# A hybrid decoder step: the chunk preparation reordered, and the sample's attention in f32r high and low parts

## The reference

```python
h = rmsnorm(x, norm_g); proj = h @ w_in            # (tokens, 1024) @ (1024, 4104)
qkv = silu(conv4(proj_a)); o_a = gated_delta_rule(q, k, v, g, beta, s0)   # 4 heads of 128, chunked
# sample's window attention, 8 heads of 64: per query t, the keys at distances 0, d, 2d, ...
parts = [dilated_branch_sample(qb, k_ext, v_ext, w // d, d) for w, d in ((128, 1), (512, 4), (2048, 16))]
o_b = merge_dilations(parts) * silu(z_b)
y = rmsnorm(x + concat(o_a, o_b) @ w_out, final_norm_g)
```

## Time and profile before

| what | value |
|---|---|
| the profiled execution's own time | 2152.05 us |
| its span, first to last instruction | 2149.3 us |
| mean granted PE clock | 0.916 |
| PE busy | 1883.7 us, 88% |
| DVE, ACT, POOL busy | 756.7, 596.1, 319.4 us |
| DMA moved | 310.31 MB, mean 144 GB/s |

### The profile page before, as it was taken

How to read it: one execution, slowest core, us unless ns; L and a number is a source line. 1 busy time by engine, 2 the same in 40 slices (tenths; PEclk the granted TensorE clock), 3 DMA queues, 4 the chain that set the end, 5 groups by cost and what they waited for, 6 DMA issues and landing times. The chain is left out here.

```text
span 2149.3 us, 29657 instructions
## 1 busy us (share of the span) xinstructions
PE 1883.7 (88%) x9726; PEld 1471.0 (68%) x9726; DVE 756.7 (35%) x1780; ACT 596.1 (28%) x1246; POOL 319.4 (15%) x351
## 2 busy tenths in 40 slices
PE   5799999999999999854659998998899559899997
PEld 4588888888888888623457887787788436555653
DVE  5541134113411431124465344444442422222331
ACT  5421132113211321111014534453445212211221
POOL 0000000000000000014313124312432331211110
PEclk9899999999999999976859888988899559999999
DMA  6234423354553234459855987797756475546560
GB/s 167 53 69 93 101 66 68 104 88 60 79 103 81 63 74 113 77 74 232 235 142 178 288 244 231 237 290 235 241 176 215 141 190 152 156 138 167 139 190 25
DMA packets 263857, 310.31 MB, mean 144 GB/s; under 512 B 69596, under 2 KB 216540, under 8 KB 254252
## 3 DMA queue, kind: packets, MB, share of 16 engines
q1 hardware_dynamic: 260148, 241.68, 46.5%
q10 hardware_dynamic: 3584, 66.98, 8.7%
HBM read 229.03 MB, written 146.44 MB: 175 GB/s over the span
## 5 line engine op out<-in xcount | busy, mean ns | idle before, releaser
L249 PE MATMUL pj<-hT_hi,w_hi 128*128 128x512 f32 (+1 forms) x1056 | 426.4, 404 | 15.1 <-DVE w_lo L446 14.5
L250 PE MATMUL pj<-hT_lo,w_hi 128*128 128x512 f32 (+1 forms) x1056 | 415.5, 393 | 0.0
L251 PE MATMUL pj<-hT_hi,w_lo 128*128 128x512 f32 (+1 forms) x1056 | 415.0, 393 | 0.0
L249 PEld LDWEIGHTS pj<-hT_hi,w_hi 128*128 128x128 f32 (+1 forms) x1056 | 197.6, 187 | 61.0 <-DVE w_lo L446 15.0
L251 PEld LDWEIGHTS pj<-hT_hi,w_lo 128*128 128x128 f32 (+1 forms) x1056 | 197.0, 187 | 47.3 <-issue 0.9
L250 PEld LDWEIGHTS pj<-hT_lo,w_hi 128*128 128x128 f32 (+1 forms) x1056 | 197.6, 187 | 41.9 <-issue 0.6
L1355 PE MATMUL o_ps<-pt,vt 128*65 128x256 f32 (+3 forms) x560 | 149.4, 394 | 3.6 <-DVE ot L1581 3.1
L586 POOL IOTA row_at<- 128x1 int32 x1 | 0.1, 138 | 945.6 <-POOLq L2339 945.6
L1422 ACT ACTIVATE pt<-pt_ps 128x512 f32<-128x512 f32 x144 | 84.6, 587 | 153.6 <-PE pt_ps L1333 152.8
L2103 PE MATMUL y_bank<-wo_hi,mh 128*128 128x512 f32 (+1 forms) x272 | 114.1, 420 | 7.4 <-POOL ml L2088 5.3
L457 DVE SCALAR_TENSOR_TENSOR acc<-raw,conv_wt,acc 128x512 f32<-128x512 f32 x144 | 108.3, 752 | 9.1 <-DVE acc L454 0.3
(11 more groups left out here) (411 smaller groups left out, 3153.9 us busy)
## 6 DMA issues: line engine op xcount, KB each, us to landing
out_dram<-in_cache_k_win_dram ACTq DMA_DIRECT2D x56, 584.0 KB, 7.2
out_dram<-in_cache_v_win_dram ACTq DMA_DIRECT2D x56, 584.0 KB, 6.0
w_raw<-in_w_in_dram SPq DMA_DIRECT2D x35, 512.0 KB, 8.5
kq<-qk_ch SPq DMA_DIRECT2D x64, 256.0 KB, 3.5
qk_ch<-sil SPq DMA_DIRECT2D x32, 256.0 KB, 2.4
z_ch<-xr SPq DMA_DIRECT2D x32, 256.0 KB, 2.5
wqk<-hi SPq DMA_DIRECT2D x32, 256.0 KB, 4.5
wqk<-lo SPq DMA_DIRECT2D x32, 256.0 KB, 3.0
```

Source lines behind the costliest of these rows:

```text
L249: pe.matmul(out, w_hi[s][:, k, 0:m], hT_hi[:, k, cols], start=(k == 0), stop=False)
L250: pe.matmul(out, w_hi[s][:, k, 0:m], hT_lo[:, k, cols], start=False, stop=False)
L251: mm = pe.matmul(out, w_lo[s][:, k, 0:m], hT_hi[:, k, cols], start=False, stop=(k == KT - 1))
```

## The change

Preparation: `g_tok` is split into high and low f32r parts, the decay is summed by two f32r products, and the mask above the diagonal is added by a third (`ident_r` times `shut`, minus 1e30), so POOL's mask after the exponential is gone. `kq` is loaded into a ring of five buffers, all five in the gates stage, with the `kq` of the first two delta chunks beside them; the ring lies in the memory of the class scores, `sc_class`. Eight near score units of the first head stand between the chunks 7 to 14. The substitution stands in the first head's order (`head_order(True, True)`): its 15 rows before the turns 1 to 8, and no delta step before unit 9; the inverse's way over DRAM follows it. `cross` is cleared after that, since the corners lie in it. The first pair of heads is written out instead of looped.

Output: keys, q, values and probabilities are each split into a high f32r part and the rest. One product takes 64 stationary columns (q high and q low) against the keys' high part, a second the 32 high ones against the keys' low part; the rows 32 to 63 are added to the rows 0 to 31 before the mask (DVE) and, for the values, by a product with `fold`. The new keys and values join the last far block. `lb` comes in groups of four tiles (1 MB), loaded after the steps 0, 2 and 4. SP's and POOL's loops are written out.

```diff
                 sp.dma_start(E.g_dn[:], D.dn_norm_g.unsqueeze(1)).then_inc(loaded, 16)
-            for e in range(2):
-                load_kq_from(sp, D, env, e, e, env.kq_in)
+            for c in range(RING):
+                load_kq_from(sp, D, env, c, env.kq_ring[c], env.ring_in[c])
             load_qk_from(sp, D, env, 0, 0)
             load_near_v_from(sp, D, env, 0)
             load_class_v_from(sp, D, env, 0)
             for e in range(2):
                 load_tokens_from(sp, D, env, e, e)
+                load_kq_from(sp, D, env, e, env.operands[5][e], env.chunk_in[e])
             load_z_from(sp, D, env, 0)
             load_qk_from(sp, D, env, 1, 1)
...
+            then(dve.tensor_copy(E.g_hi[:], g[:, 0:NT]))
+            then(dve.tensor_tensor(E.g_lo[:], g[:, 0:NT], E.g_hi[:].bitcast(F32), ALU.subtract))
...
+SUBS = 8
+FIRST_DELTA = 9
+
+
+def head_order(more, opening=False):
+
+
+
+    order, cost = [("exp", 0)], [0 if opening else 18]
 
     def add(c, *step):
         order.append(step)
         cost.append(c)
 
     for k in range(UNITS + LAG):
+        if opening and k == FIRST_DELTA:
+            cost = [0] * len(cost)
+        if opening and 0 < k <= SUBS:
+            for row in range(2 * k - 1, min(2 * k + 1, BASE)):
+                add(0, "sub", row)
+        if opening and k == SUBS:
+            add(0, "flip")
...
-                    if q < 8 and LATEST[q] + q % 2 == k or q >= 8 and LATEST[q] == k:
+                    if k == (LATEST[q] if q >= 8 else FIRST_DELTA + q // 2 if opening else LATEST[q] + q % 2):
...
-FIRST_SCORES = [("score", q) for q in range(UNITS)] + [("spread",), ("swap",), ("peak",)]
+FIRST_SCORES = [("score", q) for q in range(8, UNITS)] + [("spread",), ("swap",), ("peak",)]
+RING = 5
+EARLY = {NT - 9 + q: q for q in range(8)}
...
-                sp.wait_ge(S["kq_mm"], 2 * c + 2)
-                if c + 2 < NT:
-                    load_kq_from(sp, D, env, c + 2, e, kq_in)
-                else:
-                    load_kq_from(sp, D, env, e, e, chunk_in)
+                if c + RING < NT:
+                    sp.wait_ge(S["kq_mm"], 2 * c + 2)
+                    load_kq_from(sp, D, env, c + RING, ring[c % RING], ring_in[c % RING])
...
+            head(0, 0, OPENING)
+            head(0, 1, BODY[0])
+            with eng.Fori(1, PAIRS - 1) as i:
                 for e in range(2):
-                    for step, *a in BODY[0]:
-                        if step == "delta":
-                            delta(2 * i + e, a[1], a[0])
-                        else:
-                            attend(i, e, step, *a)
+                    head(i, e, BODY[0])
             for e in range(2):
-                for step, *a in BODY[e]:
-                    if step == "delta":
-                        delta(2 * (PAIRS - 1) + e, a[1], a[0])
-                    else:
-                        attend(PAIRS - 1, e, step, *a)
+                head(PAIRS - 1, e, BODY[e])
...
-            def mask(c):
-                pool.wait_ge(S["decay_exp"], c + 1)
-                pool.tensor_tensor(dec[c % 2][:], dec[c % 2][:], heads(E.upto), ALU.mult).then_inc(S["decay_masked"], 1)
-
-            build(0)
-            for c in range(1, NT):
-                build(c)
-                mask(c - 1)
-            mask(NT - 1)
+                for x, g in enumerate((E.g_hi, E.g_lo)):
+                    pool.tensor_tensor(gm[c % 2][:, x], heads(E.upto), row(g, c), ALU.mult).then_inc(S["gm_built"], 1)
...
+            pool.wait_ge(S["inv_out"], 32)
+            for e in range(2):
+                pool.memset(cross[e][:], 0.0).then_inc(S["zeroed"], 1)
...
-                pe.matmul(pt_ps[u][:], E.after[:], flat(gm[u][:]), start=True, stop=True).then_inc(S["decay_mm"], 1)
-                pe.wait_ge(kq_in[u], 16 * KQ_DMAS * (c // 2 + 1))
+                pe.matmul(pt_ps[u][:], E.ident_r[:], heads(E.shut), start=True, stop=False)
+                pe.matmul(pt_ps[u][:], E.after_r[:], flat(gm[u][:, 0]), start=False, stop=False)
+                pe.matmul(pt_ps[u][:], E.after_r[:], flat(gm[u][:, 1]), start=False, stop=True).then_inc(S["decay_mm"], 1)
+                pe.wait_ge(ring_in[c % RING], 16 * KQ_DMAS * (c // RING + 1))
...
+                if c in EARLY:
+                    score(0, 0, EARLY[c], 1)
...
-            act.wait_ge(S["sub_step"], 2 * BASE - 2)
-            act.wait_ge(S["inv_out"], 32)
...
+            load_linv_group(sp, D, lb, 0, group_in)
...
+                if b in (0, 2, 4):
+                    sp.wait_ge(O["scaled"], 2 * b + 4)
+                    load_linv_group(sp, D, lb, b // 2 + 1, group_in)
...
+            def low_v(b):
+                for i, (v, w, ts) in enumerate(PARTS[0:2]):
+                    pool.wait_ge(G["v_hi"], len(PARTS) * b + i + 1)
+                    pool.tensor_tensor(v_lo[0:w, ts, :], v[0:w, ts, :], v_hi[0:w, ts, :].bitcast(F32), ALU.subtract).then_inc(G["near_lo"], 1)
...
+            for b in range(DEC_BATCH - 1):
+                low_v(b)
+                share(2 * b + 2)
                 low(2 * b + 2, 0)
                 root(2 * b, 0, P)
                 root(2 * b + 1, 1, P)
-                share(1, b + 1)
+                share(2 * b + 3)
...
-                a = dict(start=(j == 0), stop=(j == NJ - 1))
-                pe.matmul(s_ps[0][0:ROWS, :], q(j), kT[:, j % 2, 0:NEAR], **a)
-                pe.matmul(s_ps[1][0:ROWS, 0:FARS], q(j), kT[:, j % 2, NEAR:], **a).then_inc(G["kT_used"], 1)
-                if j == NJ - 1:
-                    for k in range(NJ):
-                        mm = pe.matmul(s_ps[1][0:ROWS, FARS:FARS + T], q(k), kw[:, k, :], start=(k == 0), stop=(k == NJ - 1))
-                    mm.then_inc(G["scored"], 1)
+                both, high = (qw[:, 2 * ROWS * j:2 * ROWS * j + w] for w in (2 * ROWS, ROWS))
+                for x, (a, z) in enumerate(((0, NEAR), (NEAR, KEYS))):
+                    pe.matmul(s_ps[x][0:2 * ROWS, 0:z - a], both, kT[:, 0, j % 2, a:z], start=(j == 0), stop=False, skip_group_check=True)
+                    mm = pe.matmul(s_ps[x][0:ROWS, 0:z - a], high, kT[:, 1, j % 2, a:z], start=False, stop=(j == NJ - 1), skip_group_check=True)
+                mm.then_inc(G["kT_used"], 1)
...
-            def mix(b):
-                pe.wait_ge(v_in, 48 * b + 48)
-                pe.wait_ge(G["pT_out"], b + 1)
+            def mix(b, far):
+                pe.wait_ge(G["far_lo" if far else "near_lo"], 2 * (b + 1))
+                if not far:
+                    pe.wait_ge(G["p_lo"], b + 1)
                 pe.sem_inc(G["seen"], 1)
-                for k in range(9):
-                    v, w = (vn[:, k, :], P) if k < T else (vf[:, k - T, :], FAR) if k < 2 * T else (vnew[:], T)
-                    mm = pe.matmul(s_ps[0][0:ROWS, :], pT[0:w, ROWS * k:ROWS * k + ROWS], v, start=(k == 0), stop=(k == 8))
-                mm.then_inc(G["mixed"], 1)
+                for a, z, w in BLOCKS[1:] if far else BLOCKS[0:1]:
+                    for k in range(a, z):
+                        t = k % T
+                        pe.matmul(s_ps[0][0:2 * ROWS, :], pT[0:w, k, :], v_hi[0:w, t, :], start=(k == 0), stop=False, skip_group_check=True)
+                        mm = pe.matmul(s_ps[0][0:ROWS, :], pT[0:w, k, 0:ROWS], v_lo[0:w, t, :], start=False, stop=(k == 2 * T - 1), skip_group_check=True)
+                mm.then_inc(G["mixed" if far else "near_mixed"], 1)
...
-                    mm = pe.transpose(p_ps[:, O_AT + ROWS * j:O_AT + ROWS * j + ROWS], o_sb[:, P * j:P * j + P], ident[0:ROWS, 0:ROWS])
+                    mm = pe.matmul(p_ps[:, O_AT + ROWS * j:O_AT + ROWS * j + ROWS], o_sb[:, P * j:P * j + P], fold[:], start=True, stop=True)
...
-                mix(b)
-                half_tile(2 * b + 1, 1, 1, P)
+                mix(b, False)
+                half_tile(2 * b + 1, 1, 1, P, 0, 6)
+                mix(b, True)
+                half_tile(2 * b + 1, 1, 1, P, 6, KT)
...
-                act.activation(kT[:, j % 2, 0:NEAR], near_ps[j % 2][:], ACT.Copy).then_inc(G["kT_act"], 1)
+                act.activation(kT[:, 0, j % 2, 0:NEAR], near_ps[j % 2][:], ACT.Copy).then_inc(G["near_hi"], 1)
+                act.wait_ge(G["far_mm"], NJ * b + j + 1)
+                act.activation(kT[:, 0, j % 2, NEAR:NEAR + FARS], far_ps[j % 2][:, 0:FARS], ACT.Copy).then_inc(G["far_hi"], 1)
+
+            def split_v(b, parts):
+                for v, w, ts in parts:
+                    act.activation(v_hi[0:w, ts, :], v[0:w, ts, :], ACT.Copy).then_inc(G["v_hi"], 1)
 
             def step(b, more):
-                for j in range(NJ):
-                    turned(b, j)
+                turned(b, 0)
+                turned(b, 1)
+                act.wait_ge(v_in, 48 * b + 48)
+                split_v(b, PARTS[0:2])
+                turned(b, 2)
+                turned(b, 3)
+                act.wait_ge(G["max"], b + 1)
+                act.activation(pr[:], pr[:], ACT.Exp, bias=snmax[:, 0:1], accum_out=slsum[:, 0:1]).then_inc(G["exped"], 1)
```

(32 more changed lines are left out.)

233 lines of the change are left out of this document (131 added, 102 removed).

## The result

| | before | after |
|---|---|---|
| median of 9 runs each | 2158.59 us | 2147.42 us |
| lowest to highest | 2151.65 to 2168.09 | 2141.12 to 2149.90 |
| the profiled execution | 2152.05 us, span 2149.3 | 2144.46 us, span 2142.7 |
| mean granted PE clock | 0.916 | 0.903 |

A forecast was written before the change was run, and what follows sets the result against it. Bounds: DMA engines in gates and chunk preparation, DVE from there to the first head, PE in the output stage. 2152.05 - 14.5 ((a) to (c)) - 28.5 (output) = 2109.05, given as 2110 us; range 2080 to 2142.

The forecast's parts named there:

- (a): Gates stage: SP's ten kq loads add 7 us, cross memsets of 2.70 us leave POOL's way; first chunk 4.3 us later.
- (c): Chunks to first head: first cross product 7.5 us earlier, 10 us of head work done ahead, 3 us charged for delta steps.
- (b): Preparation: with the DMA queue kept full, the last chunk ends at 1054 instead of 1062 us, a gain of 8 to 9.
- (d): Output stage, sample's attention on PE: f32r products for scores and mix save 7.3 us of a step.
- (e): Output stage, split's cost on other engines: +2.2 us before the first score, -0.7 before the probabilities, +0.85 clock, per step.
- (f): Output stage, ACT's new wait for values: none normally, 2.1 us every second step, +1.0 average; first step's late gf +5.
- The slower clock takes over: Rival, chance 0.07: projection matmuls in each output step run at 1.2 GHz after waits, 11.2 us a step, total 2186.
- The values come late: Rival, chance 0.17: values land 5.5 us after PE's need in seven output steps, the stage gains nothing, total 2147.
- The rule at the q copies: Output step: DVE copies beside POOL's subtraction would cost 2.2 us more; left out, as POOL ends at 7.4, copies start 9.4.

The follow-up runs named there:

- mix_only: Preparation and heads of the changed kernel with the output stage of the kernel before: 2142.28 us, ratio 0.9935 to the kernel before.
- best1: Changed kernel with the three edits of split_late, linv_behind and early_q together: 2081.12 us, ratio 0.9650 to the kernel before.
- out_only2: Preparation and heads of the kernel before with the output stage of the changed kernel: 2154.62 us, ratio 1.0000 to the kernel before.
- split_late: Changed kernel, but ScalarE splits the near values behind key blocks 2 and 3, not between 1 and 2: 2120.18 us, ratio 0.9821 to the kernel before.
- linv_behind: Changed kernel, but the 1 MB linv load is issued behind the loads of x, values and first-step gf: 2120.64 us, ratio 0.9829 to the kernel before.
- early_q: Changed kernel, but VectorE's q copies precede key blocks 0 and 1, and its gf wait precedes gf's first use: 2133.91 us, ratio 0.9889 to the kernel before.
- keys_on_act: Changed kernel, but ScalarE instead of VectorE copies the new keys into each key block: 2130.13 us, ratio 0.9880 to the kernel before.
- best3: best2, but the next step's q copies stand in VectorE's pause before the exponential is ready: 2077.19 us, ratio 0.9630 to the kernel before.
- best2: best1, but ScalarE's high part of the odd tile moves behind key blocks 0 and 1 of the next step: 2079.98 us, ratio 0.9637 to the kernel before.

## Why the prediction was wrong, point by point

**(a) to (c), right in the sum, less so in the parts.** SP issued ten loads in 7.99 us where 7 to 8 were counted; the first chunk started at 993.4, 4.8 us later (4.3 forecast). The first exponential was at 1066.1 (1068), the inverse stored at 1085.5 (1088), the first cross product at 1104.2 (1105.5). The round trip took 18.7 us from the store (17.8 forecast). But the last chunk was done at 1049.9 us, 4 us before the 1054 of (b) and just outside its 1050 to 1058, and the way from there to the exponential took 16.2 us and not 14.1. And (c) had 7.5 us at the first cross product and 7 more in the head behind it: measured are 8.9 and 3.7. That these misses partly cancel is luck. The sum was -14.5; 12.55 in the traces and 14 us in mix_only.

**(d), right at the full clock.** It said 7.3 us less PE work in a step. best1, with the clock at 0.99, has (256.24 - 210.33) / 6 = 7.7 less, a part of it the clock, which was 0.97 before.

**(e), its first wait right, its clock too small.** The wait before the first score is 2.43 us (2.9 forecast). Before the probabilities it is 4.0 us over seven steps where 13.3 were counted: where the half clock behind score 3 makes PE late (steps 3, 4 and 6) there is none, and in best1 it is 1.5 us a step or a little more (1.9 forecast). The clock was counted at 0.85 us a step; it costs 2.9 against best1. Steps 1 to 6 of each trace (the last two columns over steps 1 to 7: the 3.2 us behind the wait before score 0):

| | PE's work | idle | wait before score 0 | slow behind it |
|---|---|---|---|---|
| changed | 227.5 us | 50.2 us | 2.4 us | 5 of 7 steps |
| out_only2 | 225.5 | 48.7 | 2.4 | 6 of 7 |
| split_late | 225.9 | 30.1 | 2.4 | 5 of 7 |
| linv_behind | 223.3 | 36.4 | 2.4 | 5 of 7 |
| early_q | 221.1 | 54.8 | 1.5 | none |
| keys_on_act | 219.6 | 46.0 | 1.8 (0.35 in step 7) | none |
| best1 | 210.3 | 20.5 | 1.5 | none |

"Slow" is a mean granted clock of 0.52 to 0.72; in all other steps it is 1.00. So the clock did not only follow from (f): with (f)'s waits gone, split_late got back 1.6 us, and early_q, which has more idle time than the changed kernel, 6.4. The wait of 2.4 us that (e) had foreseen costs clock of its own; 1.5 us at the same place cost none. All 17 us came back only when both were shorter. *The slower clock takes over* was the rival with this mechanism; the size that it gave (2186) was not reached.

**(f), the step that failed.** It said no wait in even steps and 2.1 us in odd ones, 7 us in all; the traces show 34.3. Three sizes were off, in step 3: the values landed at 22.3 us and not at 17.4; the copies of the new keys added 1 us to the first block; and PE was there at 20.1 us and not 19.0. The wait worked out again is 2.1 + 4.9 + 1.0 - 1.1 = 6.9, the row's 6.87. The landing had been counted on the best 9 us of the queue, 316 GB/s; over the 18 us that the loads took, the changed kernel moved 244 GB/s (306 in the middle). And the second block, which DVE makes 2.3 us behind the first (1.34 + 0.68 + 0.54, less their overlap) while PE scores a block in 1.0 us at the full clock, was not in the count at all: it is the 1.32 us of the even steps. The first step's late `gf` was seen (+5; it was 6.4), but not what DVE has to do behind it: from `gf` to the last q copy it took 5.9 us (1760.63 to 1766.52) where it had taken 1.5, and 3.0 of that are two copies of 0.16 us that stood beside POOL (2.02 and 1.32). That made the wait 11.3 us longer on PE.

That is *The values come late*, given 0.17: it asked for a landing 5.5 us after the need in seven steps and gave 2147. The wait measured is 4.9 us on the average of seven, and the time 2147. That the figure agrees to the microsecond is in part luck: the clock and the first step took more than it had, the other waits less.

**The rule at the q copies.** The prediction left out the 2.2 us that copies beside POOL would cost, because POOL had ended. At that place it was right (0.50 us). But the change gave POOL a new operation, 4.66 us for the near values, and DVE's copies of the new keys stand beside it: 0.88 and 1.34 us for 0.16, the second ending at 1917.48 with POOL's at 1917.45. keys_on_act prices these copies at 14 us of the whole, with the clock. The shared port of the Trainium skill (SBUF — State Buffer, Who interferes with whom), which a two-port DVE operation and a GpSimd operation hold in turn, agrees with these rows; it was applied to the operation that was there before and not to the one that was added.

**The sum**, for steps 1 to 7 of the traces: waits before scores 2 and 3 +34.3, before score 0 +11.9, before the probabilities -11.7, the tail -0.6, PE's work -32.6, together +1.3; it was forecast at -27.7. Of the 29 us between the two, (f)'s waits are 27.3 and PE's work, through the clock, 12.6; the wait before score 0 gave back 3.5, that before the probabilities 6.8 and the tail 0.6. The first step is 4.6 us longer where 1.5 less were forecast.

## What to carry to other kernels

When an engine gets a new wait in the middle of its list, price its landing by the slowest stretch of the queue with everything ahead of it, and then put the waiting instruction behind whatever does not need it: here two moved blocks of code are worth 50 us, more than four times what the whole change had brought. Look for the wait in the order of each engine, and not only at the operation that needs the data: `gf` was needed 30 us after the place where DVE waited for it. An idle time of some microseconds on PE can cost more than itself, because the work behind it may run at 1.2 GHz: before score 2, waits of 6.3 us and more did so each time (12 steps of four kernels); before score 0, waits of 2.4 us did in 21 of 28 steps and waits of 1.4 to 1.8 us in none of 27.

## What the runs showed of the hardware

In these traces a plain copy on DVE that stands beside POOL's two-operand instruction lasts to its end, even one of 8 elements a partition: 0.16 us became 2.30 (it ended at 1865.77 in best3, POOL at 1865.75), and four q copies, 0.50 us alone, became 2.65. The scaling by a scalar (0.68) took 2.15 in one step of split_late. Subtractions with an operand in PSUM were the same beside POOL, 0.68 us for 512 columns. The price of a small copy is thus the rest of POOL's instruction, so moving it to another pause helps only where POOL is idle (best3).

The granted clock behind a wait of PE differed with the wait's length. Before score 0 it was 1.00 behind each of 27 waits of 1.4 to 1.8 us (early_q, keys_on_act, best1, best2), and 0.52 to 0.72 over the next 3.2 us behind 21 of 28 waits of 2.4 us (the changed kernel, out_only2, split_late, linv_behind). The length is not all: before the probabilities in best1, where every wait is 1.5 to 1.9 us, it was 0.58 and 0.79 behind two of eight. What decides these was not tried.
